# A mixture of 32 experts: blocks of 32 tokens on four column tiles, tokens picked by TensorE instead of gathered

## The chip, the core and the metric

The kernel runs on one core of a Trainium2 chip as one launch. The metric is the device time of a run in microseconds, lower is better. All data is float32; batch 1, 512 tokens, width 1024.

## What is computed

The reference is two layers. The first is a gated mixer (GMLP and HGRN2) followed by a mixture of experts; the second a convolution layer and a dilated attention layer. The change touches only the mixture of experts:

```python
g_idx = jnp.argmax(g_logits, axis=-1)                  # 1 of 4 groups
top_v, top_i = lax.top_k(e_logits, 2)                  # 2 of its 8 experts
wts = g_prob[:, None] * jax.nn.softmax(top_v, axis=-1)
eid = (g_idx[:, None] * 8 + top_i).reshape(-1)         # 1024 assignments
# for each expert e, on its tokens xb (n, 1024):
h = jax.nn.silu(xb @ w_gate[e]) * (xb @ w_up[e])       # (n, 512)
out = h @ w_down[e]                                    # (n, 1024)
# y[token] = sum over its two experts of weight * out
```

Each of the 32 experts has three 2 MB weight matrices (201 MB together). The routing of the reference's own inputs gives the experts 41, 44, 16, 16, 19, 41, 36, 41, 15, 33, 16, 15, 31, 10, 20, 14, 60, 30, 39, 81, 69, 53, 41, 39, 20, 21, 27, 31, 25, 23, 34 and 23 assignments, in the order in which the kernel takes them.

## The kernel before

**Blocks and slots.** Every expert has a first block of `CAP` = 64 token slots; a second block runs only if the expert has more than 64 assignments, and for more still there are up to `NOV` = 12 overflow blocks that load their weights again. Which blocks run is read from a small table `ctl` (`read_ctl`, L749) by each engine, and blocks that don't run are skipped by branches whose other side keeps the semaphores counting.

**Before the experts.** ACT writes the normed tokens `xs` to DRAM (`xn_scratch`, L949). DVE works out for each of the 1024 assignments its slot (L1510 to L1586), then the tables `Jm` and `Bm` (L1594, L1597), which TensorE multiplies to the list of tokens of every slot (`tab_i`, L1602).

**One expert, n.** POOL gathers the 64 rows of the block from `xn_scratch` by an indirect DMA (`gather`, L1934). PE turns them in eight transposes (`turn_x`, L523), DVE scales them by the norm's gain (`scale_x`, L1622). `up` (L529) multiplies with the gate and up weights, two panels side by side on two column tiles of 64: 16 calls of 512 columns. ACT takes the silu (`silu_gate`, L958), DVE the product (`gated`, L1626), PE turns it (`turn_h`, L535), ACT copies it (`copy_h`, L961), `down` (L539) multiplies with the third panel in 8 calls, ACT copies the result out (`copy_y`, L964), and SP stores it to `y_scratch` in two halves (`store`, L2037). The copy of block n waits until the store of block n-2 has landed; second blocks have a single output buffer, so their copy waits for the landing of the second store before. A float32 call of `mm` (L283) shows as two weight loads and two matmul records in the profile.

**What sets the order.** All weight panels are loaded by SP (`load`, L1997; the issue is L2007) in the order of use, into nine slots of 2 MB each: four of the ring, two of the area `ar`, three of `spare`. A panel's load waits until its slot's former panel has been used: the ups (`m_up`, `o_up`) for the first two panels of an expert, the downs (`m_d2`, `o_d2`) for the third. The stores are issued by SP too, between the loads, and run through the same hardware queue. The first eight panels are requested during the routing, the ninth after the first gather has landed.

**After the experts.** POOL gathers each token's two results from `y_scratch` in eight indirect DMAs (L1980), once all stores have landed; the second layer follows.

## Time and profile before

| | us |
|---|---|
| runs | 1606.17, 1610.14, 1611.7 (median 1610.14) |
| profiled execution | 1606.9 |
| its span | 1605.2 |
| busy PE / PEld / DVE / ACT / POOL | 1391.7 / 941.1 / 659.7 / 479.2 / 84.9 |
| mean granted TensorE clock | 0.942 of full |

Times in the rows are microseconds from the start of the span. A row of the timeline gives start, duration, engine, line, operation, output<-inputs and count, and in brackets the idle time before it with what ended it. PEclk is the granted clock (1.00 is 2.4 GHz, 0.50 is 1.2 GHz). A DMA share is the mean busy share of the core's 16 DMA engines.

### The profile page before, as it was taken

Reading aid. Unit: us, or ns where it says so; the run is one execution under the profiler, and the core shown is the slowest. Engines: PE = TensorE matmul, PEld = TensorE weight load, DVE = VectorE, ACT = ScalarE, POOL = GpSimd, SP = SyncE. Lnnn points to the kernel's source line nnn. Section 1 sums busy time; section 2 is a strip of 40 time slices with the busy share of each in tenths; the row PEclk is TensorE's granted clock in tenths of the full one; section 3 lists DMA queues with packets and bytes.
Section 4 is the critical chain, followed back from the end, with each engine's and each line's share of the span. In section 5 each row is a group of like instructions: output and inputs, shape, how many; then the busy total and the mean of one; then the engine's idle time right before and its main releaser. Section 6 shows DMA issues by size and latency. Waiting matters only on the chain.

```text
span 1605.2 us, 17082 instructions
## 1 busy us (share of the span) xinstructions
PE 1391.7 (87%) x6498; PEld 941.1 (59%) x6498; DVE 659.7 (41%) x1144; ACT 479.2 (30%) x709; POOL 84.9 (5%) x139
## 2 busy tenths in 40 slices
PE   6999995997767779976828999988999999999986
PEld 5787774332222323322317888766888888888765
DVE  4477746000000000000054756455266566666635
ACT  5462521100000001100153221324344445444532
POOL 2010001110000000100020010000000000000000
PEclk9999996999888989998959999989999999999988
DMA  8737428999999999999973553211212121121101
GB/s 351 319 130 252 168 105 312 334 379 404 390 402 405 399 375 395 391 393 392 396 297 131 210 210 131 70 64 53 105 53 106 53 103 56 53 105 53 53 1 65
DMA packets 41002, 347.68 MB, mean 217 GB/s; under 512 B 6080, under 2 KB 6208, under 8 KB 22592
## 3 DMA queue, kind: packets, MB, share of 16 engines
q1 hardware_dynamic: 29632, 304.69, 48.8%
q0 software_dynamic: 10304, 38.84, 7.0%
q10 hardware_dynamic: 960, 2.70, 0.5%
q8 instruction: 72, 1.18, 0.3%
q14 instruction: 34, 0.28, 0.0%
HBM read 321.56 MB, written 24.64 MB: 216 GB/s over the span
## 4 chain that ended last, share of the span: by engine, by line
PE 49%; DVE 3%; ACT 2%; issue 2%; DMA 1%; DVEq 0%; SPq 0%; ACTq 0%; POOLq 0%
PE ps L283 48%; PE ps L676 1%; ACT ar L818 1%; DVE b_NL L1252 0%; DMA ar<-y_scratch,rt 0%; DVE ar L1244 0%; DVE hres L1679 0%; DVE hres L1686 0%; ACT b_NH L827 0%; PE ps L289 0%; DVE ar L1869 0%; ACT ar L1032 0%; DVE ar L1203 0%; ACT ar L962 0%; DMA y_scratch<-ar 0%
## 5 line engine op out<-in xcount | busy, mean ns | idle before, releaser
L283 PE MATMUL ps<-ring,ar 128*64 128x512 f32 x720 | 259.6, 624 | 64.6 <-issue 54.1
L283 PE MATMUL ps<-ar 128*64 128x512 f32 (+5 forms) x766 | 253.2, 488 | 8.7 <-DVE ar L1597 4.6
L1627 DVE TENSOR_TENSOR ar<-ar,ps 128x256 f32<-128x256 f32 x34 | 14.3, 421 | 478.8 <-ACT ar L959 465.9
L283 PEld LDWEIGHTS ps<-ring,ar 128*64 128x64 f32 x720 | 76.8, 143 | 221.7 <-issue 207.1
L283 PE MATMUL ps<-b_NH,b_WH 128*128 128x512 f32 x704 | 186.9, 401 | 9.7 <-DVE b_NL L1252 5.0
L283 PE MATMUL ps<-b_NH,b_WL 128*128 128x512 f32 x704 | 181.3, 393 | 0.0
L1185 DVE TENSOR_TENSOR b_WL<-ring,b_WH 128x1024 fp32r<-128x1024 f32 x112 | 136.6, 1221 | 100.9 <-ACT b_WH L770 100.9
L283 PE MATMUL ps<-b_NL,b_WH 128*128 128x512 f32 x704 | 173.9, 390 | 0.0
L770 ACT ACTIVATE b_WH<-ring 128x1024 fp32r<-128x1024 f32 x112 | 118.1, 1055 | 162.3 <-PE ps L283 159.9
L283 PEld LDWEIGHTS ps<-b_NH,b_WH 128*128 128x128 f32 x704 | 130.6, 190 | 38.3 <-ACT b_NH L827 9.9
L283 PEld LDWEIGHTS ps<-b_NH,b_WL 128*128 128x128 f32 x704 | 133.7, 190 | 28.0
L283 PE MATMUL ps<-spare,ar 128*64 128x512 f32 x544 | 128.6, 627 | 24.0 <-issue 17.6
L283 PEld LDWEIGHTS ps<-b_NL,b_WH 128*128 128x128 f32 x704 | 132.5, 188 | 27.6
L283 PEld LDWEIGHTS ps<-ar 128*64 128x64 f32 (+3 forms) x766 | 102.9, 168 | 34.6 <-issue 20.8
L965 ACT ACTIVATE ar<-ps 128x512 f32<-128x512 f32 x34 | 20.3, 597 | 338.9 <-DMA y_scratch<-ar 305.1
L283 PEld LDWEIGHTS ps<-spare,ar 128*64 128x64 f32 x544 | 41.6, 143 | 102.5 <-issue 93.4
L289 PE MATMUL ps<-ident,ar 128*128 128x128 f32 x128 | 23.2, 351 | 49.4 <-ACT ar L1036 28.9
L1798 DVE TENSOR_TENSOR ar<-ps,gate 128x512 f32<-128x512 f32 x48 | 33.2, 691 | 78.2 <-ACT ar L1111 77.9
L1185 DVE TENSOR_TENSOR a_WL<-ring,a_WH 128x1024 fp32r<-128x1024 f32 x32 | 39.3, 1231 | 54.8 <-ACT a_WH L770 54.8
L283 PE MATMUL ps<-a_WH,a_NH 128*128 128x512 f32 x192 | 55.7, 398 | 3.5 <-DVE a_NL L1432 2.3
L1110 ACT ACTIVATE ar<-ps 64x512 f32<-64x512 f32 x48 | 28.5, 594 | 99.3 <-PE ps L283 98.6
L283 PE MATMUL ps<-b_WH,b_NH 128*128 128x512 f32 x192 | 55.7, 397 | 1.4 <-ACT b_NH L1088 1.4
(260 smaller groups left out, 1671.9 us busy)
## 6 DMA issues: line engine op xcount, KB each, us to landing
ring<-in_wts_dram SPq DMA_DIRECT2D x79, 2048.0 KB
spare<-in_wts_dram SPq DMA_DIRECT2D x31, 2048.0 KB, 39.8
ar<-in_wts_dram SPq DMA_DIRECT2D x22, 2048.0 KB
ring<-in_wmod_dram SPq DMA_DIRECT2D x24, 512.0 KB, 4.6
ar<-in_wmod_dram POOLq DMA_DIRECT2D x24, 512.0 KB, 4.1
y_scratch<-gate POOLq DMA_DIRECT2D x11, 1024.0 KB, 21.5
y_scratch<-ar SPq DMA_DIRECT2D x68, 128.0 KB, 32.1
hres<-in_x_dram SPq DMA_DIRECT2D x4, 512.0 KB, 6.4
```

Source lines behind the costliest of these rows:

```text
L283: return pe.matmul(o, l, m, start=start, stop=stop, skip_group_check=True)
L289: t = pe.transpose(ps[:, banks[k], p * 128:(p + 1) * 128], x[:, p, k * 128:(k + 1) * 128], ident[:, :])
L676: t = pe.transpose(ps[:, 4, q * 128:(q + 1) * 128], Sb[p % 2][:, q * 128:(q + 1) * 128], ident[:, :])
L770: act.activation(chunk_dst(buf, c, feat), chunk_src(i, n), ACT.Copy).then_inc(S["hi"], 1)
L818: act.activation(o, src, ACT.Identity, scale=mcol[:, l, 0, k:k + 1], bias=mcol[:, l, 1, k:k + 1]).then_inc(S["tta"], 1)
L965: return act.activation(ysb[s], ps[:, b, :], ACT.Copy)
L1110: act.activation(w[0:64, :], o[64:128, :], ACT.Copy)
L1185: dve.tensor_tensor(chunk_dst(ops[3], c, feat), chunk_src(i, n), f32(chunk_dst(ops[2], c, feat)), ALU.subtract).then_inc(S["lo"], 1)
L1627: return dve.tensor_tensor(hh[s], sg[s], ps[:, b, 256:512], ALU.mult)
L1798: dve.tensor_tensor(q, o, cosT, ALU.mult).then_inc(S["ra"], 1)
```

## The change

Blocks have 32 slots. An expert has a first block, a second above 32 assignments, a third above 64, and up to 26 overflow blocks beyond (`NOV`). Up and down run on four column tiles of 32, with 256 columns a call: 32 calls in `up`, 16 in `down`; the weight panels are laid out on the host to match. No tokens are written to DRAM or gathered: the normed tokens `xs` stay in SBUF, where the ninth weight slot was, and DVE writes for a group of four experts a matrix `OH` of ones and noughts (512 tokens by 128 first slots and 128 second slots); TensorE multiplies `xs` with it. For the first four experts the first slots are picked before the loop and the second slots inside expert 0, one pair of feature tiles at a time; for the later groups a quarter of the picking is done in each expert (`pick_both`: 8 calls of 256 columns). A third block picks its own tokens (`pick_one`: 32 calls of 32 columns) and runs at the end of its expert; SP stores it before it asks for the next panels. A block's result is stored in one transfer, written as four quarters of 256 columns. POOL reads its branch table at the very end, before it gathers the results. The order of the DVE steps that find the slots is a little shorter, with 15 thresholds instead of 7.

```diff
-CAP = 64
-NOV = 12
-NBLK = 2 * NE + NOV
-NSLOT = NBLK * CAP
+CAP = 32
+NOV = 26
+NSLOT = (3 * NE + NOV) * CAP
...
-        slots = [ring[:, j, :] for j in range(RING)] + [area(4096, 4096), area(0, 4096)] + [spare[:, j, :] for j in range(3)]
+        slots = [ring[:, j, :] for j in range(RING)] + [area(4096, 4096)] + [spare[:, j, :] for j in range(3)]
...
+            def pick_main(u, b):
+                for k in (2 * u, 2 * u + 1):
+                    for p in range(4):
+                        t = mm(ps[:, b, (k % 2) * 128:(k % 2) * 128 + 128], xs[:, p, k * 128:(k + 1) * 128],
+                               OH[:, p, 0:128], p == 0, p == 3)
+                return t
...
+            def pick_both(u, b):
+                for k in (2 * u, 2 * u + 1):
+                    for p in range(4):
+                        t = mm(ps[:, b, (k % 2) * 256:(k % 2) * 256 + 256], xs[:, p, k * 128:(k + 1) * 128],
+                               OH[:, p, :], p == 0, p == 3)
+                return t
...
+            def pick_one(b):
                 for k in range(8):
-                    t = pe.transpose(ps[:, b, k * 64:(k + 1) * 64], xg[s][0:64, k * 128:(k + 1) * 128],
-                                     ident[0:64, 0:64])
+                    for p in range(4):
+                        t = mm(ps[:, b, k * 32:(k + 1) * 32], xs[:, p, k * 128:(k + 1) * 128], OH3[:, p, :],
+                               p == 0, p == 3)
                 return t
...
-            def up(s, b, pan):
+            def up(x, b, pan):
                 for k in range(8):
-                    mm(ps[0:64, b, :], xT[s][:, k, :], pan[0][:, k * 512:(k + 1) * 512], k == 0, k == 7)
-                    t = mm(ps[64:128, b, :], xT[s][:, k, :], pan[1][:, k * 512:(k + 1) * 512], k == 0, k == 7)
+                    for j in range(4):
+                        t = mm(ps[32 * j:32 * j + 32, b, 0:256], x[:, k, :],
+                               pan[j // 2][:, k * 512 + (j % 2) * 256:k * 512 + (j % 2) * 256 + 256], k == 0, k == 7)
                 return t
...
-                    lh = hT[s][:, q % 2, (q // 2) * 64:(q // 2) * 64 + 64]
-                    mm(ps[0:64, b, :], lh, pan[:, q * 1024:q * 1024 + 512], q == 0, q == 3)
-                    t = mm(ps[64:128, b, :], lh, pan[:, q * 1024 + 512:(q + 1) * 1024], q == 0, q == 3)
+                    for j in range(4):
+                        t = mm(ps[32 * j:32 * j + 32, b, 0:256], hT[s][:, q, :],
+                               pan[:, q * 1024 + j * 256:q * 1024 + j * 256 + 256], q == 0, q == 3)
                 return t
...
+            for u in range(4):
+                pe.wait_ge(S["m_oh"], 1)
+                if u == 3:
+                    pe.wait_ge(S["m_xt"], 1)
+                pick_main(u, (3, 7, 5, 3)[u]).then_inc(S["m_gx"], 1)
...
+                q0, e0 = 32 * (n % 4), n // 4
+                x = xTg[e0 % 2]
                 pe.wait_ge(s_slot[place[i]], landing[i])
                 pe.wait_ge(s_slot[place[i + 1]], landing[i + 1])
-                pe.wait_ge(S["m_xt"], n + 1)
-                if n:
-                    pe.wait_ge(S["m_hh"], n)
-                up(s, 0, (panel(i), panel(i + 1))).then_inc(S["m_up"], 1)
+                pe.wait_ge(S["m_xt"], 4 if n < 4 else 4 * e0 + 8)
+                if n >= 2:
+                    pe.wait_ge(S["m_hh"], n - 1)
+                up(x[:, :, q0:q0 + 32], 2 - s, (panel(i), panel(i + 1))).then_inc(S["m_up"], 1)
+                if n == 0:
+                    pe.wait_ge(S["m_oh"], 2)
+                    for u in range(4):
+                        if u:
+                            pe.wait_ge(S["m_xt"], 4 + u)
+                        else:
+                            pe.wait_ge(S["m_xt"], 4)
+                        pick_second(u, 3).then_inc(S["m_gx"], 1)
+                    pe.wait_ge(S["m_xt"], 8)
+                    pe.wait_ge(S["mpd"], 5)
                 with pe.If(second(n)):
-                    pe.wait_ge(S["o_g"], 16 * (n + 1))
                     if n:
-                        pe.wait_ge(S["o_xt"], n)
                         pe.wait_ge(S["o_hh"], n)
-                    turn_x(2, 1).then_inc(S["o_tx"], 1)
-                    pe.wait_ge(S["o_xt"], n + 1)
-                    up(2, 2, (panel(i), panel(i + 1))).then_inc(S["o_up"], 1)
+                    up(x[:, :, 128 + q0:160 + q0], 0, (panel(i), panel(i + 1))).then_inc(S["o_up"], 1)
                 with pe.Else():
                     if n:
-                        pe.wait_ge(S["o_tx"], n)
                         pe.wait_ge(S["o_up"], n)
-                    pe.sem_inc(S["o_tx"], 1)
                     pe.sem_inc(S["o_up"], 1)
-                if n + 1 < NE:
-                    pe.wait_ge(S[f"g{(n + 1) % 2}"], 16 * ((n + 1) // 2 + 1))
-                    turn_x(1 - s, 3).then_inc(S["m_tx"], 1)
+                if n + 4 < NE:
+                    pe.wait_ge(S["m_oh"], n // 4 + 3)
+                    pe.wait_ge(S["m_xt"], 8 + n)
+                    pick_both(n % 4, 3).then_inc(S["m_gx"], 1)
...
+                with pe.If(third(n)):
+                    pe.wait_ge(S["m_xt"], min(9 + n, NE + 4))
+                    pe.wait_ge(S["o_hh"], n + 1)
+                    pe.wait_ge(S["o_ht"], n + 1)
+                    pe.wait_ge(S["o_y"], n + 1)
+                    pe.wait_ge(S["t_oh"], n + 1)
+                    pick_one(3).then_inc(S["t_gx"], 1)
+                    pe.wait_ge(S["t_xt"], n + 1)
+                    up(xT3, 0, (panel(i), panel(i + 1))).then_inc(S["t_up"], 1)
+                    pe.wait_ge(S["t_hh"], n + 1)
+                    turn_h(3, 6).then_inc(S["t_d1"], 1)
+                    pe.wait_ge(S["t_ht"], n + 1)
+                    down(3, 7, panel(i + 2)).then_inc(S["t_d2"], 1)
+                    pe.wait_ge(S["t_y"], n + 1)
...
+                with act.If(third(n)):
+                    act.wait_ge(S["t_up"], n + 1)
+                    if n:
+                        act.wait_ge(S["t_hh"], n)
+                    silu_gate(3, 0).then_inc(S["t_sg"], 1)
+                    act.wait_ge(S["t_d1"], n + 1)
+                    copy_h(3, 6).then_inc(S["t_ht"], 1)
+                    act.wait_ge(S["t_d2"], n + 1)
+                    if n:
+                        act.wait_ge(S["ty"], 16 * n)
+                    copy_y(3, 7).then_inc(S["t_y"], 1)
...
+            def pick_in(g, cl, o, sem):
+                dve.tensor_scalar(rel, sl_f, float(-g), None, ALU.add).then_inc(S["m_e"], 1)
+                for p in range(4):
+                    if p == 0:
+                        dve.wait_ge(S["m_e"], n_e[0] + 1)
+                    dve.tensor_scalar(o[:, p, cl], i256[:, cl], rel[:, p:p + 1], None, ALU.is_equal).then_inc(S["m_e"], 1)
+                n_e[0] += 5
+                for p in range(4):
+                    dve.wait_ge(S["m_e"], n_e[0] - 3 + p)
+                    t = dve.scalar_tensor_tensor(out=o[:, p, cl], in0=i256[:, cl], scalar=rel[:, 4 + p:5 + p],
+                                                 in1=o[:, p, cl], op0=ALU.is_equal, op1=ALU.add)
+                t.then_inc(S[sem], 1)
...
+            for u in range(4):
+                dve.wait_ge(S["m_gx"], u + 1)
+                scale_x(xTg[0], (3, 7, 5, 3)[u], 2 * u, 0, 128).then_inc(S["m_xt"], 1)
+            pick_in(0, slice(128, 256), OH, "m_oh")
             mod_end(0)
-            signals(dve.tensor_tensor(t1_, m2, m1, ALU.subtract), "gexp")
+            for u in range(4):
+                dve.wait_ge(S["m_gx"], u + 5)
+                scale_x(xTg[0], 3, 2 * u, 128, 128).then_inc(S["m_xt"], 1)
+            pick_in(128, slice(0, 256), OH, "m_oh")
...
+            def third_block(u, slot0):
+                dve.tensor_scalar(rel, sl_f, float(-slot0), None, ALU.add).then_inc(S["t_e"], 1)
+                dve.wait_ge(S["t_e"], 5 * u + 1)
+                if u:
+                    dve.wait_ge(S["t_gx"], u)
+                for p in range(4):
+                    dve.tensor_scalar(OH3[:, p, :], i256[:, 0:32], rel[:, p:p + 1], None,
+                                      ALU.is_equal).then_inc(S["t_e"], 1)
+                for p in range(4):
+                    dve.wait_ge(S["t_e"], 5 * u + 2 + p)
+                    t = dve.scalar_tensor_tensor(out=OH3[:, p, :], in0=i256[:, 0:32], scalar=rel[:, 4 + p:5 + p],
+                                                 in1=OH3[:, p, :], op0=ALU.is_equal, op1=ALU.add)
+                t.then_inc(S["t_oh"], 1)
+                dve.wait_ge(S["t_gx"], u + 1)
+                if u:
+                    dve.wait_ge(S["t_up"], u)
+                dve.tensor_tensor(xT3, ps[:, 3, 0:256].rearrange("p (k j) -> p k j", k=8),
+                                  bc(last(cols[:, C_G2:C_G2 + 8]), 128, 8, 32), ALU.mult).then_inc(S["t_xt"], 1)
+                dve.wait_ge(S["t_sg"], u + 1)
+                if u:
+                    dve.wait_ge(S["t_d1"], u)
+                gated(3, 0).then_inc(S["t_hh"], 1)
...
+                if n % 4 == 3 and n + 5 < NE:
+                    pick_in(128 * (n // 4 + 2), slice(0, 256), OH, "m_oh")
...
+            pool.wait_ge(S["slot"], 1)
+            pool.wait_ge(S["ovx"], 1)
+            pool.wait_ge(S["m_d2"], NE)
+            pool.wait_ge(S["m_y"], NE)
+            pool.wait_ge(S["y0"], 16 * (NE // 2))
+            pool.wait_ge(S["y1"], 16 * (NE // 2))
+            pool.wait_ge(S["oy"], 16 * NE)
+            pool.wait_ge(S["ty"], 16 * NE)
+            pool.wait_ge(S["yzero"], 16 * 12)
+            n_over, second, third = read_ctl(pool)
             for j in range(NOV):
                 with pool.If(n_over > j):
-                    if j == 0:
-                        pool.wait_ge(S["o_tx"], NE)
-                    else:
-                        pool.wait_ge(S["o_tx"], NE + j)
-                    pool.wait_ge(S["o_g"], 16 * (NE + j))
-                    gather(2, 2 * NE + j).then_inc(S["o_g"], 16)
-                    pool.wait_ge(S["oy"], 32 * (NE + j + 1))
-            pool.wait_ge(S["m_d2"], NE)
-            pool.wait_ge(S["m_y"], NE)
-            pool.wait_ge(S["y0"], 32 * (NE // 2))
-            pool.wait_ge(S["y1"], 32 * (NE // 2))
-            pool.wait_ge(S["oy"], 32 * NE)
-            pool.wait_ge(S["yzero"], 16 * 11)
+                    pool.wait_ge(S["ty"], 16 * (NE + j + 1))
...
             def store(n, s):
-                for hf in range(2):
-                    t = sp.dma_start(y_d[n * CAP:(n + 1) * CAP, hf * 512:(hf + 1) * 512],
-                                     ysb[s][64 * hf:64 * hf + 64, :])
-                    yield t
+                return sp.dma_start(y_d[n * CAP:(n + 1) * CAP, :].rearrange("t (q c) -> q t c", q=4),
+                                    ysb[s])
             for n in range(NE):
+                with sp.If(third(n)):
+                    sp.wait_ge(S["t_y"], n + 1)
+                    if n:
+                        sp.wait_ge(S["ty"], 16 * n)
+                    store(2 * NE + n, 3).then_inc(S["ty"], 16)
+                with sp.Else():
+                    if n:
+                        sp.wait_ge(S["ty"], 16 * n)
+                    sp.sem_inc(S["ty"], 16)
                 for m in range(3):
-                    i = P_MOE + 3 * n + m + 9
+                    i = P_MOE + 3 * n + m + 8
                     if i < P_C0:
```

## Rows read from the trace of the kernel before

**Rows 1.** The page's 40 slices of the span: DMA busy tenths, GB/s.
```profile
DMA  8737428999999999999973553211212121121101
GB/s 351 319 130 252 168 105 312 334 379 404 390 402 405 399 375 395 391 393 392 396 297 131 210 210 131 70 64 53 105 53 106 53 103 56 53 105 53 53 1 65
```

**Rows 2.** Windows of 40 us: PE, PEld, DVE, ACT, POOL busy (x), PEclk, DMA share, GB/s.
```profile
340.00:380.00 40.00, 31.82 (x146) 11.18 (x144) 2.22 (x4) 2.62 (x6) 2.87 (x4) 0.92 1.01 387
620.00:660.00 40.00, 36.86 (x184) 13.13 (x186) 3.70 (x7) 4.36 (x10) 4.30 (x6) 1.00 1.01 400
```

**Rows 3.** DMA queues in 295 to 795 us: packets, MB, share of 16 engines.
```profile
q1 hardware_dynamic: 17351, 188.90, 95.4%
q0 software_dynamic: 3313, 7.91, 5.1%
```

**Rows 4.** DMA in 463.5 to 472.5 us, no gather under way.
```profile
DMA packets 420, 3.89 MB, mean 432 GB/s; under 512 B 90, under 2 KB 90, under 8 KB 196
```

**Rows 5.** DMA in 457 to 463.5 us, one gather under way.
```profile
DMA packets 237, 2.24 MB, mean 345 GB/s; under 512 B 33, under 2 KB 33, under 8 KB 119
...
q1 hardware_dynamic: 157, 1.96, 85.9%
```

**Rows 6.** The page's groups: the gate product, once a block.
```profile
L1627 DVE TENSOR_TENSOR ar<-ar,ps 128x256 f32<-128x256 f32 x34 | 14.3, 421 | 478.8 <-ACT ar L959 465.9
```

**Rows 7.** Timeline before and at the first expert: start us, us.
```profile
266.40 0.69 DVE L1594 TENSOR_TENSOR ar<-ar 128x512 f32<-128x512 f32 x1
267.01 1.92 DVE L1597 TENSOR_SCALAR ar<-ar,rt 128x76 f32<-128x76 f32 x8
...
275.83 11.36 SPq L2007 DMA_DIRECT2D ring<-in_wts_dram  x2
...
287.28 0.38 SPq L2007 DMA_DIRECT2D ar<-in_wts_dram  x1
```

**Rows 8.** Windows at the start of the experts, columns as in rows 2.
```profile
270.00:275.00 5.00, 0.00 (x0) 0.00 (x0) 3.54 (x14) 0.20 (x1) 2.58 (x3) 0.50 0.27 76
275.00:280.00 5.00, 3.11 (x14) 1.78 (x16) 0.69 (x1) 0.00 (x0) 0.91 (x1) 0.50 0.82 262
285.00:290.00 5.00, 2.91 (x20) 1.17 (x16) 1.11 (x2) 2.05 (x3) 0.91 (x1) 1.00 0.43 118
```

**Rows 9.** Stores to y_scratch: us to landing (DMA issues), and ACT waiting for one (timeline).
```profile
y_scratch<-ar SPq DMA_DIRECT2D x2, 128.0 KB, 32.4
...
589.87 0.60 ACT L965 ACTIVATE ar<-ps 128x512 f32<-128x512 f32 x1 [17.08 <-DMA y_scratch<-ar]
```

**Rows 10.** Timeline of PE inside one up product: start us, us.
```profile
563.30 0.59 PE L283 MATMUL ps<-ring,ar 128*64 128x512 f32 x1
...
563.34 0.59 PE L283 MATMUL ps<-ar 128*64 128x512 f32 x1
...
563.73 0.59 PE L283 MATMUL ps<-ring,ar 128*64 128x512 f32 x1
```

**Rows 11.** PE's groups by form (busy us, mean ns), and eight transposes in the timeline.
```profile
L283 PE MATMUL ps<-ones,ar 128*128 128x1 f32 x32 | 3.8, 252 | 0.0
...
569.87 0.70 PE L525 MATMUL ps<-ident,ar 64*128 64x64 f32 x8
```

**Rows 12.** Timeline at the end of the last expert: start us, us.
```profile
792.06 0.61 PE L283 MATMUL ps<-ring,ar 128*64 128x512 f32 x1 [2.70 <-issue]
...
800.99 3.65 PE L283 MATMUL ps<-spare,ar 128*64 128x512 f32 x16 [0.47 <-ACT ar L962]
...
804.69 0.60 ACT L965 ACTIVATE ar<-ps 128x512 f32<-128x512 f32 x1 [3.75 <-PE ps L283]
807.18 2.00 ACT L770 ACTIVATE b_WH<-ring 128x1024 fp32r<-128x1024 f32 x2 [1.89 <-issue]
...
809.84 1.66 POOL L1980 DMA_INDIRECT ar<-y_scratch,rt  x1 [28.86 <-DMA y_scratch<-ar]
```

More of the change, by code:

```diff
@@ L68, in program @@
         s_un = [ctx.enter_context(nc.semaphore(f"s_un{p}")) for p in range(4)]
-        s_slot = [ctx.enter_context(nc.semaphore(f"s_slot{j}")) for j in range(9)]
+        s_slot = [ctx.enter_context(nc.semaphore(f"s_slot{j}")) for j in range(8)]
         s_yg = [ctx.enter_context(nc.semaphore(f"s_yg{m}")) for m in range(8)]
@@ L598, in tensor_program @@
                     pe.sem_inc(S["o_d2"], 1)
+                with pe.If(third(n)):
[12 more added lines that the diff above has]
+                    pe.wait_ge(S["t_y"], n + 1)
+                with pe.Else():
+                    if n:
+                        for v in ("t_gx", "t_up", "t_d1", "t_d2"):
+                            pe.wait_ge(S[v], n)
+                    for v in ("t_gx", "t_up", "t_d1", "t_d2"):
+                        pe.sem_inc(S[v], 1)
             for j in range(NOV):
@@ L751, in read_ctl, with second, third @@
             n_over = e.value_load(ctl[0:1, 0:1], min_val=0, max_val=NOV)
-            bits = [e.value_load(ctl[0:1, 13 + j:14 + j], min_val=0, max_val=65535) for j in range(2)]
-            return n_over, lambda n: (bits[n // 16] & (1 << (n % 16))) > 0
+            bits = [e.value_load(ctl[0:1, 28 + j:29 + j], min_val=0, max_val=65535) for j in range(4)]
+            def second(n):
+                return (bits[2 * (n // 16)] & (1 << (n % 16))) > 0
+            def third(n):
+                return (bits[2 * (n // 16) + 1] & (1 << (n % 16))) > 0
+            return n_over, second, third
         def scalar_program(act):
@@ L1450, in mod_end @@
                     g = gate[:, l, 512 * c:512 * c + 512]
-                    dve.tensor_tensor(g, ps[:, 1 + c, :], g, ALU.add).then_inc(S["mpd"], 1)
+                    dve.tensor_tensor(g, ps[:, (1, 2 if l else 6)[c], :], g, ALU.add).then_inc(S["mpd"], 1)
             def residual(c, j):
@@ L1581, in vector_program @@
             behind()
[L1582 removed]
+            signals(dve.tensor_tensor(sc_, sc_, vc, ALU.add))
+            signals(dve.tensor_tensor(p1, p1, pc, ALU.add))
             behind()
[L1584 to L1589 removed]
@@ L1590, in vector_program @@
-            signals(dve.tensor_copy(gs8, blk_f.bitcast(I32)))
-            behind()
-            signals(dve.scalar_tensor_tensor(out=lo_f, in0=gs8, scalar=float(-CAP), in1=sl_f, op0=ALU.mult, op1=ALU.add))
-            behind()
-            signals(dve.tensor_tensor(Jm, bc(last(lo_f), 128, 8, CAP), bc(mid(i_n[:, 0:CAP]), 128, 8, CAP),
-                                      ALU.is_equal), "jb")
-            for c in range(8):
-                signals(dve.tensor_scalar(Bm[:, c, :], i_n, gs8[:, c:c + 1], tokid[:, c % 4:c % 4 + 1], ALU.is_equal,
-                                          ALU.mult), "jb")
@@ L1931, in gpsimd_program @@
                                channel_multiplier=-1).then_inc(S["pc"], 1)
-            def gather(s, n):
-                return pool.indirect_dma_start(
-                    out=xg[s][0:64, :], out_offset=None, in_=xn_d,
-                    in_offset=bass.IndirectOffsetOnAxis(ap=tab_i[0:64, n:n + 1], axis=0))
-            pool.wait_ge(S["ctl"], 1)
-            n_over, second = read_ctl(pool)
-            pool.wait_ge(S["tab"], 1)
-            pool.wait_ge(S["xn"], 16)
-            for n in range(2):
-                gather(n, n).then_inc(S[f"g{n}"], 16)
@@ L2050, in sync_program @@
                 sp.wait_ge(S["m_y"], n + 1)
-                for t in store(n, n % 2):
-                    t.then_inc(S[f"y{n % 2}"], 16)
+                store(n, n % 2).then_inc(S[f"y{n % 2}"], 16)
                 with sp.If(second(n)):
```

336 lines of the change are left out of this document (156 added, 180 removed).

## The prediction

> **What bounds it now.** I read the page's 40 slices first. From the eighth slice to the twentieth the DMA engines are full and the rate stays near 400 GB/s [rows 1]: this is the expert stage, about 300 to 800 us, and only a change there can matter much. The 40 us windows say the same in numbers: DMA share 1.01 while PE has 8 us of 40 free, and still 1.01 where two experts with second blocks leave PE only 3 [rows 2]. So the stage lasts as long as its transfers, and PE's work counts only where it delays a request.
>
> What do the transfers cost? Over 500 us the SP queue moved 188.90 MB and POOL's queue 7.91 MB [rows 3]. In nine microseconds without a gather in flight, but with the tail of a store, the rate was 432 GB/s [rows 4]. At it one weight panel (2.097 MB) takes 4.85 us, and 188.9 MB takes 437 us; the other 63 us of the 500 belong to some 30 gathers, 2.1 us each. One gather by itself agrees: in 6.5 us only 1.96 MB of weights passed, worth 4.5 us, so it cost 2.0 us [rows 5]. I take 2.05. A 64-row gather of 0.26 MB costs more than three times its bytes, and this is what the change can win.
>
> **The transfers, part by part.** The span is 1605.2 us and the profiled execution took 1606.9; the median of the runs, 1610.1, is 3.2 more, which I add at the end.
>
> Gathers: 31 of them lie in the full stretch; gone, they give 31 x 2.05 = -63.5 us.
>
> Stores: each of the 34 blocks [rows 6] now sends 262 KB. Afterwards the reference's own routing gives 14 experts more than 32 assignments, two of these more than 64, none more than 96: 48 blocks, no overflow, 131 KB each. By bytes that is 33 x 0.61 = 20.0 us before and 48 x 0.30 = 14.6 after, -5.4. But the new store writes `t (q c) -> q t c`: outermost on the DRAM side are only four column quarters. The trace has no transfer with fewer than 16 outermost rows, so its price has two ends. Spread over 16 engines it is 0.30 us. If a transfer is dealt out along its outermost dimension it fills four queues with 32 KB each, at 1/16 of 432 GB/s 1.21 us, and since every panel needs all 16 queues the stream goes at the pace of those four: 48 x 1.21 = 58.2, +38.2. I take the second, because the source's 128 partitions and the destination's four quarters have only four equal shares in common; the first is my main rival. The Trainium skill ("DMA: Bandwidth & Descriptors", section "Why a DMA increments its semaphore by 16 and not by 1") says that a transfer uses the largest number of engines up to 16 that divides the slowest dimension of both sides, here four; no row of this trace shows it.
>
> Start of the stage: with nine slots the ninth panel is requested at 275.8 and the tenth at 287.3, after the first up product [rows 7]; DMA idles 270 to 275 and partly around 285 [rows 8]. Afterwards there are eight slots, and the ninth panel waits for up and second up of expert 0, which has 41 assignments. Slots are known at about 266, as now (one step before L1594). Nine DVE operations make the first ones and noughts (L1597 needs 1.92 us for eight smaller ones [rows 7]): 2.4 us, 268.4. The main picks are 32 calls, each two records: 64 at 0.113 us (below), 7.2 us, but PE is at half clock at 275 [rows 8] and I put 10: 278.5. Up 3.5: 282. The second picks are 64 records again and four hand-overs through one bank, 0.9 each: 10.8, so 293. Second up: 296.5. Against 287.3 for the tenth panel now, and with one panel more to fetch: +9.2 +4.9, and 3 us for the gaps until the requests are ahead again. This is at its lowest 8, if PE is warm and the hand-overs hide; at its highest 22.
>
> Third blocks: two. Their branch on SP waits for the block's output before the next three panels are requested. Their start waits too: ACT's copy of the second block needs the previous second store landed, and a store lands some 32 us after its issue, behind the panels queued before it [rows 9]; ACT already waited 17 us for one there. So a third block begins when the queue has just run dry, and its whole chain is DMA idle time: pick 64 records x 0.113 = 7.2, turn-over 0.5, up 3.5, gate 1.2, transpose and copy 0.9, down 1.8, copy and store 1.0 = 16, and 2 for the clock that falls in the wait. Two of them: +36 (0 if the requests are far enough ahead, 40 if cold).
>
> Sum at the stream's end: -63.5 +38.2 +9.2 +4.9 +3 +36 = +28.
>
> **PE.** A call is two records, and the two column tiles run side by side: records of one tile are 0.43 us apart, of the two tiles 0.04 [rows 10]; sixteen such steps are an up product of 6.9 us, eight a down product of 3.65 [rows 12]. Four tiles of 256 columns should then give 0.054 us a record: up (64) 3.5 instead of 6.9, down (32) 1.75 instead of 3.65. Whether PE can start them so fast is not shown: the nearest rows are 32 records with one column each in 3.8 us, 0.113 apart, bound by loads of 128 columns, and eight transposes in 0.70, 0.06 apart [rows 11]. I take 0.054 to 0.065. A plain expert then needs about 10 us with its 3.5 of picking, one with a second block 16.5, the two with thirds 33: 18 x 10 + 12 x 16.5 + 2 x 33 = 444, beside some 505 of transfers. Covered, except as above. DVE and ACT work on smaller tiles and stay covered by the same transfers.
>
> **The end.** Now the last up and down products and their hand-overs take 12.6 us after PE's last wait for a panel [rows 12]; with 3.5 and 1.75 some 5 less, and I put -4 for a colder clock. Then POOL: now it issues the first of the output gathers 5.2 us after ACT's last copy began [rows 12]. The change puts its five register loads and 26 branches behind the last store. ACT needs up to 1.9 us for its twelve branches today [rows 12], so 26 are some 4, with the loads 5 (2 to 8): +5.
>
> Total: +28 -4 +5 = +29; 1610.1 + 29 = 1639. Nothing else in the kernel moves; that the 2 MB write of the normed tokens goes costs and wins nothing, as DMA is idle around it.
>
> **Rivals.**
> A, the forecast: 1639, by itself 1625 to 1652. Chance 0.45.
> B, the stores spread over all engines: 43.6 less, 1595; 1588 to 1607 with the bounds of start and thirds. This is the case on the other side. It speaks for it that all transfers of the trace seem evenly spread; it decides below 0.6 us a store, where the sum crosses zero. Chance 0.27.
> C, PE can't issue small records at 0.054. Each step of 0.01 adds about 46 us to PE's 444 (4,608 records). It passes the transfers' 505 at about 0.067; at 0.08 the stage is PE's and the end 1645 to 1675; at the 0.113 of the nearest row it is past 1740. For it: no row shows a sustained faster rate. Against: the 0.04 between tiles. Chance 0.2, two thirds of it below 1675. Of the skill, "TensorE: Matmul & The Clock Gate" (Part 1) speaks for C: with hardware decoding off the sequencer spends about 62 ns per matmul; the 0.04 us between tiles speaks against that here, unless they were queued beforehand.
> D, a start or a chain that I mis-sized by more than its bounds, 1610 to 1625: 0.08.
>
> **Range and chances.** A and B whole and the lower part of C: 1592 to 1665. About 0.3% (4.8 us) is what a measurement can tell from no change. Faster: most of B, 0.24. Same: the rest of B and some of D, 0.08. Slower: A, C and the rest, 0.68.
>
> **What would show it.** In the changed profile: no indirect transfers before the output gathers; a clean GB/s of 430 in stretches without stores. If stores use four queues, the DMA share stays below 0.95 while weights still limit and store stretches dip; if not, the period of plain experts is close to 15 us. Two holes in DMA of 15 us or more after experts 19 and 20, and one of 25 us before about 297. Up of one block 3.5 us for 64 records; if 5 or more, C. POOL's first output gather 10 us behind ACT's last copy. I am wrong if the stage ends before 795 or PE never waits for a panel.

## The result, and the profile after

The changed kernel takes 1838.6 us in the median of 4 runs (1833.1 to 1841.6), beside 1610.9 (1606.2 to 1615.1) for the kernel before: 1.141 times as long, 95% interval 1.137 to 1.146. The prediction said 1639 and 1592 to 1665. Slower was right; 200 of the 228 us were not in it.

The profiled execution took 1841.6 us, its span is 1839.7. The page of the changed kernel, its slices of PE's clock, DMA share and GB/s, and then its DMA queues (packets, MB, share of 16 engines):

```profile
PEclk9998989888787888787885589999799999999988
DMA  8745353886798863388846015532022212112101
GB/s 353 283 150 193 138 228 145 335 356 278 310 361 351 320 244 144 152 363 345 357 179 250 6 68 213 200 115 92 25 92 92 78 60 92 65 73 92 46 1 57
...
q1 hardware_dynamic: 30528, 302.07, 41.9%
q0 software_dynamic: 6704, 30.15, 4.7%
q8 instruction: 165, 2.70, 0.6%
```

Against [rows 1] the full stretch is gone. DMA is at 6 to 9 tenths where it was always at 9, it falls to 3 in two slices (the third blocks, as foreseen), and there is a slice with nothing at all, 6 GB/s at about 1030 us, which the prediction did not have. The queue to read is q8, by which the engines fetch their own instructions: 165 packets of 16 KB, where the page of before has 72.

The same windows as in [rows 2], and one at the new hole (PE, PEld, DVE, ACT, POOL busy, PEclk, DMA share, GB/s):

```profile
340.00:380.00 40.00, 27.36 (x272) 17.11 (x265) 5.14 (x14) 2.16 (x7) 0.00 (x0) 0.80 0.86 337
620.00:660.00 40.00, 25.89 (x312) 14.81 (x310) 1.96 (x4) 2.43 (x8) 0.00 (x0) 0.83 0.78 318
...
1020.00:1060.00 40.00, 0.00 (x0) 0.00 (x0) 0.00 (x0) 0.00 (x0) 0.00 (x0) 0.50 0.03 5
```

Neither PE (26 us of 40) nor DMA (0.78) is full, so something between them sets the pace. From 1020 to 1060 no engine at all is busy. PE's waits from 280 to 1090 us name it (line waited for: us in total, times, longest):

```profile
PE ps L283 <- PEq L649: 156.7, 28, 6.7
PE ps L289 <- issue: 111.7, 1, 111.7
PE ps L283 <- ACT ar L1018: 18.2, 48, 0.4
```

PEq is PE's own sequencer. L649 is the `sem_inc` in the Else of `third(n)`: 28 times, after an expert without a third block, the matrix unit stands still while its sequencer gets from the branch to the Else, past a body that isn't run. 26 of these waits last 4.9 to 6.7 us, 6.0 on average; the other two are short. No line waits for a panel any more. PE's timeline at one plain expert, and at the end of the last:

```profile
565.24 1.93 PE L283 MATMUL ps<-ar 128*32 128x256 f32 x32 [0.37 <-ACT ar L1018]
573.40 5.65 PE L283 MATMUL ps<-ring,ar 128*32 128x256 f32 x64 [6.23 <-PEq L649]
...
954.49 1.93 PE L283 MATMUL ps<-ring,ar 128*32 128x256 f32 x32 [0.37 <-ACT ar L1018]
1068.16 5.76 PE L289 MATMUL ps<-ident,ar 128*128 128x128 f32 x32 [111.73 <-issue]
```

A down product takes 1.93 us, then come 6.23 us of nothing, and the next up product runs at half clock (5.65 for 64 records; where nothing stood still before it, the same 64 take 3.5 to 3.7). What PE waits for in those 6 us shows in q8: each of the 26 waits holds exactly one of its packets (567.2 to 573.4: one), and in all 26 PE goes on 3 to 4.4 us after that packet starts. In the kernel before, the 14 waits of over 1.8 us put down to issue hold four such packets together and ten of them none, as waits for panels would.

After the last expert PE needs 111.7 us to pass 26 overflow bodies, none of which runs. The convolution's input was ready long before: ACT began to write its last quarter at 998.4.

### The profile page after: what moved, and what is told of

It is laid out like the page before. It is cut to its first block and busy times, and to the rows that moved or that the text cites. A ratio compares the mean times of both kernels' runs of the same rounds, so it can differ in the third digit from the quotient of the medians.

```text
span 1839.7 us, 24617 instructions
## 1 busy us (share of the span) xinstructions
PE 1450.7 (79%) x9870; PEld 1093.3 (59%) x9870; DVE 684.4 (37%) x1250; ACT 477.7 (26%) x751; POOL 39.3 (2%) x75
## 2 busy tenths in 40 slices
DMA packets 37875, 335.90 MB, mean 183 GB/s; under 512 B 3680, under 2 KB 9952, under 8 KB 19360
## 3 DMA queue, kind: packets, MB, share of 16 engines
q0 software_dynamic: 6704, 30.15, 4.7%
## 5 line engine op out<-in xcount | busy, mean ns | idle before, releaser
L283 PE MATMUL ps<-ar 128*32 128x256 f32 (+7 forms) x1662 | 291.2, 394 | 46.2 <-PEq L649 24.8
L283 PE MATMUL ps<-ring,ar 128*32 128x256 f32 x2304 | 225.0, 451 | 90.2 <-PEq L649 72.0
L283 PEld LDWEIGHTS ps<-ar 128*128 128x128 f32 (+4 forms) x1662 | 206.9, 179 | 115.9 <-issue 81.3
L283 PEld LDWEIGHTS ps<-ring,ar 128*32 128x32 f32 x2304 | 113.7, 129 | 160.2 <-issue 116.1
L283 PE MATMUL ps<-spare,ar 128*32 128x256 f32 x1728 | 150.2, 442 | 68.5 <-PEq L649 59.8
L1684 DVE TENSOR_TENSOR ar<-ar,ps 128x128 f32<-128x128 f32 x48 | 13.8, 288 | 477.7 <-ACT ar L1015 474.5
L283 PEld LDWEIGHTS ps<-spare,ar 128*32 128x32 f32 x1728 | 75.8, 126 | 122.5 <-issue 89.6
L289 PE MATMUL ps<-ident,ar 128*128 128x128 f32 x128 | 22.8, 351 | 132.4 <-issue 111.7
L1015 ACT ACTIVATE ar<-ps 128x128 f32<-128x128 f32 x48 | 13.3, 278 | 422.3 <-PE ps L283 422.3
L289 PEld LDWEIGHTS ps<-ident,ar 128*128 128x128 f32 x128 | 20.2, 186 | 136.4 <-issue 129.6
(257 smaller groups left out, 1615.1 us busy)
```

The costliest lines, as they stand in the source:

```text
L283: return pe.matmul(o, l, m, start=start, stop=stop, skip_group_check=True)
L289: t = pe.transpose(ps[:, banks[k], p * 128:(p + 1) * 128], x[:, p, k * 128:(k + 1) * 128], ident[:, :])
L1015: return act.activation(sg[s], ps[:, b, 0:128], ACT.Silu)
L1684: return dve.tensor_tensor(hh[s], sg[s], ps[:, b, 128:256], ALU.mult)
```

## The experiments

All are made from the changed kernel. Medians are of 4 to 7 runs each, unless a run is called a single one, where I read nothing under 5 us. The kernel before ran beside each and stayed at 1608.7 to 1611.8.

**One jump over the overflow.** Only PE's program changes.

```diff
-            for j in range(NOV):
-                with pe.If(n_over > j):
+            with pe.If(n_over > 0):
+                for j in range(NOV):
+                    with pe.If(n_over > j):
```

> Edit: on TensorE alone the 26 overflow bodies stand inside one outer branch, so that with no overflow block there is one jump past all of them and not 26; every other engine keeps its 26. Theory F (TensorE's instruction stream: a jump over a long body that isn't taken costs some us each, 111.7 us for the 26 in the changed kernel's trace): TensorE reaches the turn of the convolution's input when ScalarE and VectorE have it ready, near 1000 us and not near 1080, so about 80 us less: 1755 to 1765 us. Rival W (TensorE waits there for something else that comes late, the first outputs' gather or the ring's loads, and the branches only stand beside it): within 5 us of the changed kernel, 1834 to 1844 us.

1767.9 us, 70.7 less. PE's second wait became

```profile
PE ps L289 <- ACT ar L1106: 36.9, 3, 33.5
```

that is, it waits for its input again and no longer for itself. q8 fell from 165 to 134 packets: 26 bodies passed one by one had cost 31 fetches, and the one far jump leaves the code between unfetched. 111.7 us of waiting became 36.9, so 75 is what could come back, not the 80 that I had put; the time is 3 us above the range given.

**Short bodies where no third block runs.** The branch stays, its bit is read, and only experts 19 and 20, which take a third block in this input, keep the long body.

```diff
                 with pe.If(third(n)):
-                    pe.wait_ge(S["m_xt"], min(9 + n, NE + 4))
+                    if n not in (19, 20):
+                        pe.wait_ge(S["t_y"], n + 1)
+                    else:
+                        pe.wait_ge(S["m_xt"], min(9 + n, NE + 4))
...
```

> Edit: the branch for a third block stays at all 32 experts on TensorE, read from the same bits, but for the 30 experts that take no third block its body is one wait, and only experts 19 and 20 have the full body of some 160 matmuls. Theory F: the 28 idle times of up to 6.7 us behind such branches (156.7 us) go, and the main block's first product, which then starts at the higher clock, is shorter; the tail's 26 jumps stay. 1839 - 157 = 1682, less up to 30 us by the clock, not below what the transfers allow (my forecast 1639 plus the tail's 80 = 1719 if four-engine stores cost what I said): 1660 to 1720 us. Rival B (the branch itself, the read of its bit, or the hand-over of the four semaphores costs the 6 us, whatever the size of the body): 1834 to 1844. Rival S (stores on four engines bound the stage, TensorE only waits in another place): the idle time moves to the panels' waits and the time falls by under 30 us.

1741.9, 96.7 less. The branches, their reads and semaphores are all still there, so rival B has fallen; it is the length of what is jumped over. The time is above the range of theory F, 1660 to 1720. q8: 127 packets, 38 fewer for 30 bodies, so a body is 1.27 packets, about 21 KB. The waits:

```profile
PE ps L289 <- issue: 107.0, 1, 107.0
PE ps L283 <- DMA ring<-in_wts_dram: 39.3, 8, 7.6
```

Only 97 of 157 us came back, because PE now waits for panels again: the transfers took over as the bound.

**Both.**

> Edit: both of the above. Theory F: what is left is what the prediction had in its sum, 1600 to 1665 us, with 1639 the forecast itself if the store's four engines and the third blocks' holes cost what it said. If the stores by four engines cost nothing, 1595 to 1602. Rival W or B: over 1750 us.

1675.1: the two together are worth 163.5 of the 167.3 that they are worth singly. It is 10 us above the range given, and 36 us over the forecast are left.

**Both, with stores spread.**

```diff
-                return sp.dma_start(y_d[n * CAP:(n + 1) * CAP, :].rearrange("t (q c) -> q t c", q=4),
-                                    ysb[s])
+                for q in range(4):
+                    sp.dma_start(y_d[n * CAP:(n + 1) * CAP, 256 * q:256 * q + 256],
+                                 ysb[s][32 * q:32 * q + 32, :]).then_inc(S[sem], 16)
```

> Edit: both of the above, and each block's result is stored by four transfers of 32 rows of 1 KB in place of one transfer whose outermost index runs over 4. By the prediction's working one four-engine store costs 1.21 us more of the expert stage than one on sixteen engines, so this is 38 to 44 us faster than the kernel without it. Rival: the queues have slack where TensorE sets the pace, so under 10 us, and SyncE's 3 more issues for each block cost as much again.

1639.9, 35.2 less, a little under the 38 to 44 given. (That this time equals the prediction's 1639 is luck: it has other stores than the prediction's kernel, and single terms are off by up to 20 us, see below.) Windows of the kernel with both edits, and then of this one:

```profile
300.00:380.00 80.00, 70.52 (x939) 46.30 (x942) 9.82 (x25) 7.85 (x26) 0.00 (x0) 0.98 0.97 400
460.00:540.00 80.00, 50.91 (x517) 31.77 (x513) 10.69 (x28) 4.31 (x14) 0.00 (x0) 0.82 0.97 405
620.00:700.00 80.00, 61.87 (x588) 47.10 (x592) 6.91 (x25) 4.03 (x13) 0.00 (x0) 0.70 0.24 94
```

```profile
300.00:380.00 80.00, 71.39 (x956) 46.99 (x954) 9.82 (x25) 7.85 (x26) 0.00 (x0) 0.98 0.98 401
460.00:540.00 80.00, 61.81 (x634) 38.44 (x638) 8.08 (x20) 5.53 (x18) 0.00 (x0) 0.83 1.01 425
620.00:700.00 80.00, 65.41 (x784) 46.50 (x777) 8.29 (x29) 5.91 (x20) 0.00 (x0) 0.85 0.50 199
```

Where only transfers limit (460 to 540) the rate rises from 405 to 425 GB/s, at a share of 1.01. With four-quarter stores the share stays at 0.97, as it would where four engines are behind the others; the prediction had put its sign for that at below 0.95. The third window holds the third blocks: at a share of 0.24, 61 of 80 us are lost to DMA.

**A skipped body in four sizes.** The kernel with both edits, but the bodies that are never run hold the pick alone in experts 0 to 9, pick and up in 10 to 14, twice that in 15 to 17, and the whole body after.

```diff
+                    if n < 10:
+                        pick_one(3).then_inc(S["t_gx"], 1)
+                    elif n < 15:
+                        pick_one(3)
+                        up(xT3, 0, (panel(i), panel(i + 1))).then_inc(S["t_up"], 1)
+                    elif n < 18:
+                        for _ in range(2):
...
```

> Edit: the kernel with both edits, but the skipped third body has a size by expert: experts 0 to 9 the pick alone (32 matmuls, by two records and two weight loads each 128 instructions), 10 to 14 pick and up (256), 15 to 17 twice that (512), 21 to 31 the full body (324). What is read is TensorE's idle time behind each skip. Theory F1 (a block of code must be fetched when the target isn't at hand): no idle time for 128, some 4 to 6 us for 256 and 324, and hardly more for 512. Theory F2 (the sequencer goes through the skipped code at some 50 us per 1000 instructions... 6.2 us for 324, so 19 ns each): 2.4, 4.9, 9.8 and 6.2 us.

A single run, 1721.1. PE's idle time behind a skip, with what came late within the same expert's products:

```
body, instructions   experts    idle us                       mean
128                  0 to 9     0 to 0.6 nine times, 5.1 once, 1.1
                                1.7 and 1.6 in mid-product
256                  10 to 14   6.0 5.8 0.6+3.6 3.6 6.7       5.3
324 (whole)          18, 21-29  6.6 4.5 5.4 5.3 6.2 6.0 ...   5.8
512                  15 to 17   11.8 6.1 7.1                  8.3
```

Three of them in PE's timeline, behind experts 1, 11 and 15:

```profile
333.43 0.41 PE L283 MATMUL ps<-ring,ar 128*32 128x256 f32 x2 [0.64 <-issue]
...
487.55 2.79 PE L283 MATMUL ps<-spare,ar 128*32 128x256 f32 x24 [5.83 <-PEq L659]
...
561.45 0.64 PE L283 MATMUL ps<-ring,ar 128*32 128x256 f32 x2 [11.79 <-PEq L659]
```

Neither theory as written. The mean grows with size as the second says, but single values don't, and q8 shows why: the idle times of 3.6 to 6.7 us hold one packet each, those of 7.1 and 11.8 us two. So it is whole fetches that are paid. Which bodies need one or two may depend on where in a 16 KB packet they happen to lie; no run shows that.

**Four bodies behind one jump.** A first try (a single run, 1678.5) tells nothing of this: its condition, `n_over > NOV`, can never hold, and its q8 count is 96, as without the bodies, so I take it that they are not in the program at all.

> Edit: the kernel with both edits (1675.1 us), and behind every fourth expert one branch over four full third bodies that are never taken: 8 jumps over 1296 instructions each, 32 bodies in all, as many as the changed kernel skips one by one. Theory J (each jump to code that isn't at hand costs one fetch, whatever lies between): 8 idle times of 4 to 7 us, 1675 + 8 x 6 = 1723 at most, less where they hide behind the panels. Theory R (all code between is streamed, about 3.4 us for each 16 KB, 111.7 us for the 26 overflow bodies): 8 idle times of 17 to 25 us, 1800 us or more.

The repeat has `n_over > 1`:

```diff
+                if n % 4 == 3:
+                    with pe.If(n_over > 1):
+                        for _ in range(4):
+                            pick_one(3)
+                            up(xT3, 0, (panel(i), panel(i + 1)))
+                            turn_h(3, 6)
+                            down(3, 7, panel(i + 2))
```

> Edit: as e10 (four full third bodies behind one branch after every fourth expert, 8 jumps over 1296 instructions each, never taken), with a condition that the program can't settle ahead of the run; in e10 it could, and the bodies were not in the program. Against the kernel with both edits (1675.1 us). Theory J (a jump costs about one fetch, whatever lies between): 8 idle times of 4 to 7 us, 1675 to 1723 us. Theory R (all code between is streamed): 8 idle times of 17 to 25 us, 1800 us or more.

A single run, 1673.3: no slower than without the 32 bodies. Some of its jumps in PE's timeline:

```profile
352.65 3.64 PE L283 MATMUL ps<-spare,ar 128*32 128x256 f32 x32 [6.97 <-issue]
...
417.56 0.64 PE L283 MATMUL ps<-ring,ar 128*32 128x256 f32 x2 [4.34 <-issue]
...
542.82 0.64 PE L283 MATMUL ps<-ring,ar 128*32 128x256 f32 x2 [7.00 <-issue]
```

A jump over 1296 instructions (some 83 KB) costs PE 4.3 to 7.0 us, the same as one over 324, and q8 has 15 packets more for 8 jumps, not the 40 that lie between. Of the seven waits that show, the three of 4.3 to 4.9 us hold one packet and the four of 6.6 to 7.0 us two. Theory J holds, with one fetch or two for a jump. These seven, 41 us together, vanish beside transfers; 28 don't.

**A prefetch hint for the branch**, with stores spread and the overflow in one branch. Its first form is issued ahead of the down product:

```diff
-                with pe.If(third(n)):
+                hint_at = pe.mark_branch_hint_location()
...
+                pe.br_cond(third(n), f"third_{n}", f"none_{n}").branch_hint(hint_at)
+                with nc.body(f"third_{n}", valid_engines=[pe.engine]):
```

> Edit: the full third-block body stays at all 32 experts on TensorE (324 instructions by records and weight loads, nothing known ahead of the run), but its branch carries a prefetch hint that is issued before the down product of the same expert; overflow bodies in one outer branch and stores by four transfers, as in the kernel with both edits and spread stores (1639.9 us). Theory F (what costs is the fetch of the code behind the jump): with the hint the fetch runs beside the down product, 1640 to 1660 us. Rival H (the sequencer steps through the skipped instructions, or the cost is of the taken jump itself): the hint changes nothing, and the time is that kernel's plus the 97 us which the small bodies took away, 1725 to 1745 us.

1748.3, with 145.7 us of idle time in 27 waits, just above rival H's 1725 to 1745, though neither of its reasons holds: the sequencer doesn't step through what it skips (four bodies cost what one does), and a taken jump by itself costs next to nothing (128 instructions). No run has this kernel without a hint. From the first and the third experiment long bodies cost 1767.9 - 1675.1 = 92.8 us, which gives an estimate of 1733 for it. Then the hint at the expert's start, and the same with the branch turned round so that the hinted side is the far one:

> Edit: as the kernel with the hint (1748.3 us), but the hint is issued ahead of the expert's first product, some 500 instructions before the branch and not some 140. If the first hint came too late for its fetch, the idle times of about 6 us behind the 30 skipped bodies shrink: 1640 to 1700 us. If a hint does nothing for such a branch here, 1740 to 1750 us again, 27 idle times as before.

> Edit: as e9 (1729.8 us; a hint at each expert's start for the branch at its end), but the branch and the hint name the far side, the one behind the body. If the idle time is the fetch of the target: the 24 to 27 idle times of 6 us shrink, 1640 to 1690 us. If not: 1725 to 1750.

Single runs, 1729.8 and 1734.0; idle 122.2 and 122.5 us in 24 waits each. Against the late hint these are three waits fewer and 14 to 19 us less, whichever side is named; against the estimate without a hint they are nothing. So hints aren't the cure, and that they help at all isn't shown. These branches are also written by hand, with a jump more at the end of the near side, which was not tried alone.

**No third blocks.** `third(n)` compares with 65535 and never holds.

> Edit: the kernel with both edits and spread stores (1639.9 us), but no expert takes its third block (the branch is there and never true), so the tokens in third blocks of experts 19 and 20 get nothing from them: it leaves that work out. It prices the two third blocks. My prediction's term says 36 us: 1604 us. By the DMA shares of the kernel with both edits, 0.24 in 620 to 700 us, it is 60 us or more of idle transfers, of which the ring takes back what it can: 1575 to 1590 us, below the kernel before.

1583.9: the two third blocks cost 56.0 us, where the prediction had 36. Without them this form, which has both edits and spread stores too, is 27 us faster than the kernel before.

**The other engines' overflow in one branch too**, as in the first experiment.

> Edit: the kernel with both edits and spread stores (1639.9 us), with ScalarE's, VectorE's, GpSimd's and SyncE's 26 overflow bodies inside one outer branch each too. The first gather of results starts 14.1 us after ScalarE's last copy in the changed kernel and 5.2 us in the kernel before: if the 26 branches cost that, 7 to 11 us less, 1629 to 1633 us; if the landing of the last store costs it, no change.

1636.7, so 3.3 us less, where 7 to 11 or nothing was expected. The medians alone are too close to tell, but the traces agree: between ACT's last copy and POOL's first gather lie 12.8 us without this edit and 9.0 with it (14.1 in the changed kernel, 956.5 to 970.6). So their 26 branches cost 3 to 4 us. What the rest above the 5.2 us of the kernel before is was not tried.

**Third blocks early.** In the kernel of the last experiment, cut to its core:

```diff
+                with pe.If(third(n)):
+                    pick_one(7).then_inc(S["t_gx"], 1)
+                    up(xT3, 0, (panel(i), panel(i + 1))).then_inc(S["t_up"], 1)
...
+                        sp.wait_ge(S["t_d2" if m == 2 else "t_up"], n + 1)
```

The first part stands behind the second block's up product, the last line in SP's `load`. SP's wait for the third result now stands behind the loads, and DVE makes the ones and noughts ahead of its first gate product.

> Edit: the kernel with both edits, spread stores and all engines' overflow in one branch (1636.7 us), and a third block no longer runs in one piece at its expert's end: its ones and noughts are built ahead of the expert's first product, its pick and up product follow at once on the second block's, the down product comes last, and SyncE asks for the next panels as soon as the third's products have read them and not when its result is copied. The two third blocks cost 56 us in one piece (1639.9 - 1583.9). If most of that is the ring standing still while a chain of single small steps runs, a third to a half is left: 1600 to 1615 us. If it is TensorE's own work at the lower clock (pick 11 to 14 us each), 1630 to 1640.

1601.9 (7 runs, 1597.2 to 1605.1), 0.995 times the kernel before, interval 0.993 to 0.997: the only form with all the work that beats it. Its window:

```profile
620.00:700.00 80.00, 73.27 (x938) 48.96 (x938) 8.30 (x22) 7.63 (x26) 0.00 (x0) 0.96 0.78 307
```

DMA has 0.78 here instead of 0.50, and PE keeps its clock (0.96 instead of 0.85). The edit moves several things at once, and no run tells their shares. But it is no kernel to use: it knows which experts overflow.

**The same without that knowledge.** PE's code for each four experts stands twice, and one branch chooses.

```diff
+            for g in range(NE // 4):
+                with pe.If(any_third(g)):
+                    for n in range(4 * g, 4 * g + 4):
+                        expert(n, True)
+                with pe.Else():
+                    for n in range(4 * g, 4 * g + 4):
+                        expert(n, False)
```

> Edit: the early third blocks (1601.9 us), but with nothing known of the experts: TensorE's code for each four experts stands twice, with third blocks behind branches and without, and one branch on the four experts' bits chooses. Here two of eight groups take the long form and skip six third bodies in it. Theory J: 8 jumps of up to 6 us, mostly beside transfers since TensorE has 25 us of waits on ScalarE and 25 on panels in the form with known experts, and 6 skips of 6 us in the long forms, of which half shows: 1602 + 5 to 20 + 15 to 30, so 1620 to 1650. Theory R: each jump streams some 50 KB for each expert, 12 us and more for each, 1700 us or more.

1650.1 (6 runs), the upper edge of what I gave: 188 us better than the changed kernel, any routing allowed, and still 2.6% slower than before. PE's waits:

```profile
PE ps L283 <- issue: 54.7, 13, 11.8
...
PE ps L283 <- PEq L617: 23.4, 6, 7.2
```

These are 78 us of idle time, where the form before has some 17 of the same two kinds, and the time is 48 longer. Most of it shows, then: PE has too little slack beside the transfers to hide it. A hint at each far jump did nothing:

> Edit: the form with one branch for each four experts (1650.1 us), where the branch names the short form as its taken side and carries a prefetch hint for it, issued at the start of the last expert ahead of it. If the idle time is the fetch of the target and a hint can start it early, six of the eight jumps' idle times (each 5.5 to 11.8 us) shrink: 1615 to 1635 us. If the hint does nothing: 1644 to 1660.

1654.2, as given for a hint that does nothing; 46.5 us in 14 waits on issue, the longest 12.4.

## Why the prediction was wrong

The step that failed is in its part on PE: a plain expert "needs about 10 us", and 444 us "beside some 505 of transfers. Covered". I counted the instructions that run and not those that are passed over. The change puts the long body of a third block into each of 32 experts and raises the overflow bodies from 12 to 26, and I costed this code on ACT and POOL alone. In the kernel before no such cost shows: PE's twelve skips of overflow bodies lie in the 25.7 us in which it waits for ACT's norms anyway. In the 27 us around them q8 moved 4 packets. Point by point:

- **Skipped third bodies**: not in the sum. 28 waits, 156.7 us, plus a lower clock after each; worth 96.7 against what bounds next. The plain expert has 10 of work, to which come 6.2 of waiting and 2.1 that its up product takes longer at half clock. Its period was 17.9 (561.04 to 578.99 between two picks), over the 14.6 of its panels, so PE and not the transfers set the pace.
- **Skipped overflow bodies**: not in the sum, 70.7 us.
- **Stores by four quarters**: right in kind. Spreading them won 35.2 us, where 43.6 lay between the two ends. How they are dealt out shows in the page's packets under 512 B, where each transfer's semaphore updates are: 3680 after the change and 6560 with four transfers for each block, which is 60 more for each of 48 blocks. Four transfers on sixteen queues each have 64, so the one before had 4: four engines. (With fewer than 16 queues for each of the four transfers, 60 more would leave the single one none.) So the Trainium skill's rule in "DMA: Bandwidth & Descriptors", section "Why a DMA increments its semaphore by 16 and not by 1", cited in the prediction, agrees with this trace, and rival B was wrong.
- **Third blocks**: right in place and cause, too small. 56 us, not 36. SP's store issues around them lasted 46.66 us at the first and 46.14 at the second; 88.1 us of the two together are waits for ACT's copy of the third result:

```profile
669.23 46.66 SPq L2111 DMA_DIRECT2D y_scratch<-ar  x3
```

  The pick alone took 10.95 us where the clock fell to half on the way, and 13.83 at half clock throughout, not 7.2. There are only eight panel slots, so little was requested ahead. Moving pick, up product and requests forward won 34.8 of the 56, with the same work done, so most of the cost was the chain's place and not the work.
- **Start**: right. SP asked for the next panel at 298.8 in the changed kernel and at 296.6 with both edits, where 296.5 was forecast. In the windows of 10 us from 250 to 310 DMA's shares add up to 51.1 us before and to 31.5 in the kernel with spread stores: 19.6 lost, some 2 more than the 17.1 of the sum.
- **PE's pace**: right, 0.054 us a record. Up 3.5, down 1.93 with 1.75 forecast, picks of both blocks 3.72. Rival C's far end, past 1740, was nearest in time, but by luck: PE issues small records as fast as hoped, and it isn't their number that holds it up.
- **The end**: POOL's first gather came 14.1 us behind ACT's last copy, 13.0 with both edits, not 10.
- **Gathers**: gone, as forecast; q0 fell from 10304 to 6704 packets. What that was worth (63.5 us in the sum) no run prices alone.

So from 1639 to 1675.1, the form without the two unforeseen costs: thirds +20, stores -8, POOL +3, start +2, and some 7 because the full stretch with spread stores runs at 425 GB/s and not 432 (1.6% of 437 us). That makes 24 of 36; 12 stay unplaced, and the untested price of the gathers may be among them.

I had set a mark for this: "I am wrong if the stage ends before 795 or PE never waits for a panel." No wait of PE in the changed kernel's trace is put down to a panel.

## What to carry to other kernels

Code that isn't run isn't free. Here a jump past a long body stopped PE for one fetch or two, 4 to 7 us in nearly all cases, whether it passed 21 KB or 83, and short bodies (128 instructions) mostly escaped. So count the jumps past long bodies on the engine that has least slack, put rare bodies of many steps behind one outer branch, and look at the instruction queue's packets when an engine waits for its own sequencer. A rare block inside a stage that is bound by transfers should use its weights as early as it can, so that their space is free for the next ones.

## What the runs showed of the hardware that was not expected

From 957 to 1079 us, the stretch in which PE passed the 26 bodies, the instruction queue moved 35 packets. 33 of them fall before 1068, while PE stood still: one in 3.4 us. From 1020 to 1060 nothing but this queue moved at all, 13 packets in 40 us:

```profile
q8 instruction: 35, 0.57, 2.4%
```

So a row of near jumps runs at the pace of these fetches. Between bodies of 1.27 packets nearly every packet is fetched, also those jumped over; over a far jump they aren't. The Trainium skill ("Runtime: NRT & Kernel Launch", section "Instruction fetch mechanics") says that a taken branch whose target lies outside the two pages at hand forces a fetch of the target's page before execution goes on. This case agrees, with one q8 packet in each of 26 waits and 6.0 us for it on PE.

PE's clock follows: behind each such wait it was granted at half (64 records of an up product in 5.65 us), and the mean over the execution was 0.883, with 0.921 once both kinds of skip were gone. What that lower clock cost by itself was not tried; from the up products, 5.65 us instead of some 3.6, I estimate 2 us for each wait.
